# Forgetting attention: q's weights of the next pair but one made ready at the end of a body, and the contraction's units from the second slot on

## The reference, cut to what matters

```
h = rmsnorm(x, ln1); z = h @ w_in          # q, k, v of 8 heads, pool features, ...
s = q_h k_h^T / sqrt(64) + F_t - F_s        # per block of 128 queries, frame-causal
p = softmax(where(kpos <= qpos, s, -inf))
o = p @ v_h
y_pool = pool_mixer(z[:, :256])
```

## Time and profile before

| | |
|---|---|
| median of 3 runs | 2277.93 us (2275.63 to 2278.31) |
| the profiled execution | 2280.02 us |
| its span, first to last instruction | 2278.2 us |
| TensorE busy | 2162.2 us, 95% of the span |
| mean granted TensorE clock | 0.981 |
| the four bodies | from 208.9 us (end of v's last turn ahead of body 0) to about 520 us |

### The profile page before, as it was taken

How to read it: one execution, slowest core, us unless ns; L and a number is a source line. 1 busy time by engine, 2 the same in 40 slices (tenths; PEclk the granted TensorE clock), 3 DMA queues, 4 the chain that set the end, 5 groups by cost and what they waited for, 6 DMA issues and landing times. The chain is left out here.

```text
span 2278.2 us, 28795 instructions
## 1 busy us (share of the span) xinstructions
PE 2162.2 (95%) x10344; PEld 1769.0 (78%) x10344; DVE 1216.9 (53%) x1660; ACT 1014.2 (45%) x1564; POOL 627.6 (28%) x389
## 2 busy tenths in 40 slices
PE   6999999878999999999999998999999999999798
PEld 5887777757878888888888877878787787877687
DVE  5545545443332322232345466777777687776763
ACT  4434544444321222211223354566666666566651
POOL 2211132254012222222344542212222232222420
PEclk9999999989999999999999999999999999999899
DMA  3110000004321221222423341011110111101312
GB/s 116 43 37 28 26 11 28 19 19 148 111 92 66 81 74 64 74 104 81 148 92 93 137 168 65 24 37 42 37 45 29 41 41 37 37 28 65 130 65 93
DMA packets 46689, 152.40 MB, mean 67 GB/s; under 512 B 6160, under 2 KB 6576, under 8 KB 46496
## 3 DMA queue, kind: packets, MB, share of 16 engines
q1 hardware_dynamic: 43056, 138.73, 17.5%
q0 software_dynamic: 3568, 12.81, 1.7%
HBM read 132.91 MB, written 18.35 MB: 66 GB/s over the span
## 5 line engine op out<-in xcount | busy, mean ns | idle before, releaser
L214 PE MATMUL psum<-h_hi,w_hi 128*128 128x512 f32 x704 | 274.1, 389 | 1.8 <-POOL w_lo L199 1.8
L216 PE MATMUL psum<-h_hi,w_lo 128*128 128x512 f32 x704 | 273.9, 389 | 0.0
L215 PE MATMUL psum<-h_lo,w_hi 128*128 128x512 f32 x704 | 273.9, 389 | 0.0
L2556 ACT ACTIVATE diff_probs<-psum,diff_neg_max 128x1280 f32<-128x1280 f32 x128 | 170.3, 1330 | 124.7 <-DVE diff_neg_max L2783 123.5
L2783 DVE TENSOR_REDUCE diff_neg_max<-psum 128x1 f32<-128x1280 f32 x128 | 189.5, 1486 | 55.0 <-PE psum L2106 54.9
L1889 DVE SCALAR_TENSOR_TENSOR gu_ada_product<-gu_ada_w,gu_cond 128x1024 f32<-128x1024 f32 x48 | 94.2, 1963 | 213.6 <-DMA gu_ada_w<-in_ada_w 210.7
L199 POOL TENSOR_TENSOR w_lo<-w_whole,w_hi 128x1024 fp32r<-128x1024 f32 x44 | 105.9, 2409 | 367.5 <-ACT w_hi L190 367.5
L2165 PE MATMUL psum<-h_hi,w_hi 128*128 128x512 f32 x480 | 192.7, 402 | 8.5 <-DVE h_lo L1515 5.4
L2166 PE MATMUL psum<-h_lo,w_hi 128*128 128x512 f32 x480 | 189.8, 395 | 0.0
L2167 PE MATMUL psum<-h_hi,w_lo 128*128 128x512 f32 x480 | 188.8, 393 | 0.0
L2426 POOL TENSOR_SCALAR diff_probs<-diff_probs,diff_recip 128x1280 f32<-128x1280 f32 x64 | 85.9, 1343 | 280.5 <-DVE diff_probs L2800 280.5
(11 more groups left out here) (407 smaller groups left out, 4902.3 us busy)
## 6 DMA issues: line engine op xcount, KB each, us to landing
w_whole<-in_w_gu SPq DMA_DIRECT2D x44, 512.0 KB, 3.4
down_w_raw<-in_w_down SPq DMA_DIRECT2D x44, 512.0 KB, 3.4
w_whole<-in_da_w_in SPq DMA_DIRECT2D x30, 512.0 KB, 3.6
gu_ada_w<-in_ada_w SPq DMA_DIRECT2D x24, 512.0 KB, 4.2
w_whole<-in_w_in SPq DMA_DIRECT2D x23, 512.0 KB, 3.5
diff_rope_half<-in_rope SPq DMA_DIRECT2D x17, 512.0 KB, 4.1
mix<-in_x SPq DMA_DIRECT2D x8, 512.0 KB, 8.9
wo_w_whole<-in_w_o SPq DMA_DIRECT2D x8, 512.0 KB, 9.3
```

The costliest lines, as they stand in the source:

```text
L214: pe.matmul(out, wh, rh, start=(k == 0), stop=False)
L215: pe.matmul(out, wh, rl, start=False, stop=False)
L216: last = pe.matmul(out, wl, rh, start=False, stop=(k == KT - 1))
L2556: act.activation(dst, core.psum[:, 1536 * z:1536 * z + NKEY], ACT.Exp, bias=nm[:, qb % 2, z:z + 1], accum_out=rs[:, qb % 2, z:z + 1]).then ...
```

## The change

q's tile of a pair is made ready one body earlier: for pair 1 ahead of body 0, and for pair i+2 in slot 30 of body i, for which the load is already in the queue. The contraction starts in slot 1 with one unit and in slot 2 with two, and the units of the end of the list are taken away: slot 25 has three, slot 26 two, slots 27 and 28 none. The other slots keep their number, so that every unit between comes three units earlier. The last body's first pool tile takes the place of "pair 4's q" in buffer 0, the second goes to buffer 1; their loads change order, and `behind` and `pe_first` change buffers with them.

```diff
     def pool(self, j):
-        return ((1, 9, 40), (0, 12, 42))[j]
+        return ((0, 12, 42), (1, 9, 40))[j]
     def behind(self, j):
-        return ((1, 10, self.pool_done(1)), (0, 13, self.pool_done(3)))[j]
+        return ((0, 13, self.pool_done(1)), (1, 10, self.pool_done(3)))[j]
...
-    COUNT = [0, 0, 0, 3, 5, 1, 1, 1, 5, 1, 1, 1, 1, 1, 1, 2, 1, 1, 1, 1, 4, 1, 1, 1, 5, 2, 2, 2, 2, 0, 0, 0]
+    COUNT = [0, 1, 2, 3, 5, 1, 1, 1, 5, 1, 1, 1, 1, 1, 1, 2, 1, 1, 1, 1, 4, 1, 1, 1, 5, 3, 2, 0, 0, 0, 0, 0]
...
-                for j in range(2):
+                for j in (1, 0):
                     ws.load(sync, ws.pool(j), d["w_in"][1 + j, :, :])
...
-                        if more and slot in (0, 3, 11):
-                            ws.subtract_lo(pool, ws.pair(i + 1, (0, 3, 11).index(slot)))
-                        if not more and slot < 2:
-                            ws.subtract_lo(pool, ws.pool(slot))
+                        if more and slot in (3, 11):
+                            ws.subtract_lo(pool, ws.pair(i + 1, (3, 11).index(slot) + 1))
+                        if more and slot == 30:
+                            ws.subtract_lo(pool, ws.pair(i + 2, 0))
+                        if not more and slot == 1:
+                            ws.subtract_lo(pool, ws.pool(1))
...
+                ws.subtract_lo(pool, ws.pair(1, 0))
                 pairs(pool, body)
...
-                        if more and slot in (0, 3, 11):
-                            ws.round_hi(act, ws.pair(i + 1, (0, 3, 11).index(slot)))
-                        if not more and slot < 2:
-                            ws.round_hi(act, ws.pool(slot))
+                        if more and slot in (3, 11):
+                            ws.round_hi(act, ws.pair(i + 1, (3, 11).index(slot) + 1))
+                        if not more and slot == 1:
+                            ws.round_hi(act, ws.pool(1))
...
                         if slot == 30:
                             act.wait_ge(s["pv_done"], nth_pt(i, 1, 1, 3) + 3)
                             v_hi(i + 1, 0)
+                            ws.round_hi(act, ws.pair(i + 2, 0))
...
                 v_hi(0, 1)
+                ws.round_hi(act, ws.pair(1, 0))
                 pairs(act, body)
...
         for n, k in enumerate(self.EARLY):
-            b = 1 - n
+            b = n
```

## The result

The changed kernel takes 2301.26 us (median of 4 runs) against 2276.78 us for the kernel before (4 runs): ratio 1.0113, 95% interval 1.0096 to 1.0129 (the two medians alone divide to 1.0108). It is slower by 24.5 us; 2306 was forecast, with a range of 2289 to 2318. The profiled execution has a span of 2300.8 us, 22.6 us over before's.

What follows compares the result with a forecast made beforehand. TensorE's queue in program order, with its gaps, was taken as the limit. The profiled execution's 2280.0 + 16.4 (waits, tails, starts) + 11.9 (clock) = 2308.3 us; the median lies 2.1 under that execution: 2306 us, range 2289 to 2318.

Steps and rivals of the forecast that it cites:

- The mid-slot ends: Slots 4, 8, 20, 24: units wait for the bank's copy, 1.25, 1.55, 1.85 and 1.55 us; slot 24's counted in the tail.
- the estimate of 7.2 us: Twelve mid-slot ends: by the rotating-banks rule alone, one copy's duration each, 12 x 0.60 us.
- Body 0's start: Slot 1's unit waits for q's lo part and holds up scores 2 and 3: loss 3.0 us.
- Starts of bodies 1 and 2: Early weights and slot 1's unit bring score 4 earlier, counted at full clock: gain 1.4 us each.
- The tail: Slot 24's turns to v's last turn: k's rounding 4.0 us late, no units as cover, +2.3 us per body.
- The last body: At its start the idle for the pool tile goes: gain 4.6 to 4.7 us at full clock.
- The clock: New waits lower TensorE's clock in seven of twelve places, slots 8 and 24 mostly: +11.9 us.
- The stall is only the copy: Rival for the mid-slot ends: ScalarE copies at once, +5.0 us in all, 2283 us; chance 0.08.
- The bank is free in time: Rival: copy waits just replace existing TensorE waits and the tail keeps up, -4.5 us, 2273.4 us; chance 0.06.
- It falls in every place: Rival: the clock drops in all twelve places, or the tail shifts fully, +36.8 us, 2315 us; chance 0.18.
- The clock stays up: Rival: no added half-clock stretches all through, +16.4 us, 2294 us; chance 0.17.

Runs made afterwards that it cites:

- e3: Changed kernel with pieces ending with their slots, the last in slot 26 (slots 25 to 28 at 4, 4, 0, 0): 2282.4 us, 1.0029 of the kernel before.
- e4: Changed kernel, same counts, ScalarE issuing the piece's copy at the head of slots 4, 8, 20 and 24: 2285.2 us, 1.0037 of the kernel before.
- e6: As e3, but ScalarE copies the last piece in slot 27 behind k's rounding: 1.0004 of the kernel before.
- e7: As e1, with slots 25 to 28 at 3, 3, 2, 0, so the last piece ends in slot 27: 1.0005 of the kernel before.
- e1: Changed kernel with counts making every piece end with its slot, slots 25 to 28 two units each: 1.0030 of the kernel before.
- e2: q's weights made ready early as in the change, with the unit counts of before: 1.0004 of the kernel before.
- e5: Kernel before, one unit ahead of v's first multiplication in slots 5 and 21, four instead of two ahead of turns in 8 and 24: 2270.98 us, 0.9976.

## Why the prediction was right

The direction and the size held, and so did the mechanism apart from the clock: more half-clock stretches were forecast, and there were not more. Elapsed times in the two profiles, from v's last turn to slot 8's turns (L1286, L1292), to slot 24's, and to v's next last turn, changed less before (the last body: from v's last turn to the turn of its last key tile, 459.89 to 542.76 against 434.90 to 521.36):

| part | forecast, us | measured, us |
|---|---|---|
| body 0, start and slot 4 | +3.0 + 1.25 | +4.3 |
| bodies 1 and 2, start and slot 4, each | -1.4 + 1.25 | +0.6, +0.8 |
| slot 8's turns to slot 24's, three bodies, each | +1.55 + 1.85 | +3.4, +3.4, +3.4 |
| tail, each | +2.3 | +2.7, +2.8, +3.9 |
| the last body | -4.7 | -3.6 |
| sum | +16.4 | +21.5 |
| half-clock stretches, apart | +11.9 | in the parts |

The three loop bodies take (459.89 - 208.07) / 3 = 83.9 us each; 80 to 85 was forecast. The 1.1 us between 21.5 and 22.6 lie outside these parts.

**The mid-slot ends.** Forecast 1.25, 1.85, 1.55, 1.55 for slots 4, 20, 8 and 24. The rows show idle times of 1.01, 1.57, 1.31, 1.23, the same in all three bodies. The delay is 0.24 more for each: the stretch with slots 8 and 20 in it is 3.36 us longer, with 2.88 us of idle. Together the twelve are 15.3 + 2.9 = 18.2 us. e3 and e4 show it by taking the waits away in two ways. The rule of the Trainium skill on rotating banks ("Perfetto Trace Analysis", section Matmuls) names what is wrong here, and the trace agrees; the estimate of 7.2 us worked out from it was too small, since the copy stood behind the exponentials or behind two roundings in ScalarE's queue. In e4, with the copy first, 4.1 us of waits are left.

**Body 0's start.** A wait of 3 us for the lo part was forecast, 3.09 us it was.

**Starts of bodies 1 and 2.** Forecast -1.4 each, measured -0.5 to -0.7: v's last turn and the first scores ran at half clock, at the end of a stretch that began in the tail, which the step had put down separately. (-0.5 to -0.7 is the table's +0.6 and +0.8 less the 1.25 of slot 4.)

**The tail.** +2.3 was forecast and k's rounding 4.0 us late; it was 4.1 late and the tail 2.7 to 3.9 longer. e6 splits e3's, which is 2.8 too. The one of 3.9 has a half-clock stretch in slot 24's units.

**The last body.** Its idle for the pool tile went as forecast, but one stretch at half clock stayed, behind score 2's wait. Up to slot 8's turns the gain is 2.9 us (35.3 against 38.2), where 4.7 was forecast; one stretch of 3.4 us at half clock costs up to 1.7, which is about the difference. Another 0.7 comes at the body's end, which the forecast did not treat.

**The clock** is the term that was mis-sized: "I take seven, 11.9 us", over starts counted at full clock. Behind body 0's start there were four, where before there were also four (one, one and two of 3.4 us; the last window of the earlier trace rows cuts its 6.8 us off at 5.9). Against the kernel before this is no change, where the forecast had three more. Of the six pairs of waits in slots 8 and 24, which I thought the surest places, one had a drop, and slot 20 had none. What the four cost is in the table: 21.5 is about 5 us over the 16.4; at the price of 1.7 us each they would be at most 6.8. 11.9 was forecast. The forecast of 28.3 over the profiled execution was 6 us too high, against 22.6, and the three stretches that did not come are 5.1 of it by that price. The number of stretches was a guess between none and twelve, and that the median came within 5 us is in part luck.

**Rivals.** "The stall is only the copy" falls with 15.3 us of waits where ScalarE is seen busy ahead of the copy. "The bank is free in time" falls with the same line. "It falls in every place" falls with the windows. "The clock stays up" (2294 us, 7 under the median; the forecast is 5 over) is nearer to what happened in slots 8, 20 and 24 than the forecast was, but not in the tail.

**Not seen in the prediction:** that the early weights are of use only where the contraction ends earlier (slot 26 in the change; e7 shows that slot 27 is enough). I put the load down as covered and did not say by what margin. e1 and e2 showed it, and e7 by the other side.

## What to carry to other kernels

When background work with one accumulation bank is moved by a few units, look first at where each group ends inside its slot, and at what stands in front of the copy in the emptying engine's queue. A unit waiting for that copy holds up all that is behind it: here three units and, in slots 4 and 20, the slot's turns. Moving work forward takes cover away at the other end, and a load which is freed by the last unit moves with it. Before moving work across a boundary, put what is already in the queue into the waits that are there: one line did more (e5, -0.24%) than any version of the change.

## What the runs showed of the hardware that was not expected

- Two waits of 1.18 and 1.31 us with 1.1 us of transposes between left the granted clock at full level in slot 8 of all three bodies. In slot 24 the waits were 1.18 and 1.23 us; the clock stayed up in two bodies, and in the third it fell to 1.2 GHz for 3.4 us. So nearly the same waits gave both outcomes, and a forecast of single drops is a guess. The tails say the same: with short matmuls and waits of 1.54 and 0.90 us the changed kernel had a fall in two of three, and e3, with the same two waits, in none. Before, waits of 1.17 and 0.64 us with 1.3 us of short matmuls between came before the fall at body 1's start.
- The profile's idle time of TensorE before a matmul of 512 columns is less than the delay. In slot 4 the last unit's last matmul starts at 222.08 and would have let the next start 0.23 us later, at 222.31; that one starts at 223.48, 1.17 us late, with 1.01 us of idle shown. It is then 0.34 us to the matmul behind it instead of 0.23. Together that is 0.27 us over the idle time shown.
